# Three edits to a three-block layer kernel on Trainium2: recurrent-cell rows by DMA, an attention output projection by seven products, and a residual factor moved into a gate

## What is computed

```python
D = where(lower, b[:, None] - b[None, :] + i[None, :], -inf)
w_intra = exp(D - m_t[..., None])
w_inter = exp(inter - m_t)
s = einsum('bhtd,bhsd->bhts', q, k) * w_intra
num = s @ v + w_inter[..., None] * (q @ C)
```

## Time and profile before

| | |
|---|---|
| median of 3 runs | 4214.31 us (4209.85 to 4216.12) |
| the profiled execution, its own time | 4215.86 us |
| its span | 4214.1 us, mean granted clock 0.992 |
| PE | 4126.5 us busy, 98% of the span |
| PEld, DVE, ACT, POOL | 2128.0, 1640.6, 823.3, 787.9 us busy |
| chain that ended last | PE 91%, DVE 4%, ACT 1% |

### The profile page before, as it was taken

How to read it: one execution, slowest core, us unless ns; L and a number is a source line. 1 busy time by engine, 2 the same in 40 slices (tenths; PEclk the granted TensorE clock), 3 DMA queues, 4 the chain that set the end, 5 groups by cost and what they waited for, 6 DMA issues and landing times.

```text
span 4214.1 us, 46243 instructions
## 1 busy us (share of the span) xinstructions
PE 4126.5 (98%) x19608; PEld 2128.0 (50%) x19608; DVE 1640.6 (39%) x2754; ACT 823.3 (20%) x1612; POOL 787.9 (19%) x511
## 2 busy tenths in 40 slices
PE   8999999999999999999999999999999999999999
PEld 3466444444444456664444444654599344444444
DVE  3656263333333323331799431535433322222311
ACT  3124110000002113221332311633243100000000
POOL 3320052324230200000363200000100032212210
PEclk9999999999999999999999999999999999999999
DMA  5420011111111120000111121001100121111121
GB/s 203 169 79 11 30 41 49 40 50 40 40 50 46 75 80 18 28 16 30 40 40 40 40 80 50 31 28 46 61 4 24 40 80 50 40 41 50 61 94 34
DMA packets 53629, 218.50 MB, mean 52 GB/s; under 512 B 6192, under 2 KB 7728, under 8 KB 51504
## 3 DMA queue, kind: packets, MB, share of 16 engines
q1 hardware_dynamic: 47520, 167.53, 11.5%
q0 software_dynamic: 5904, 48.01, 3.0%
HBM read 194.50 MB, written 18.89 MB: 51 GB/s over the span
## 4 chain that ended last, share of the span: by engine, by line
PE 91%; DVE 4%; ACT 1%; issue 1%; DMA 1%; POOL 1%; SPq 0%; DVEq 0%; POOLq 0%; ACTq 0%
PE bank L718 34%; PE bank L184 27%; PE bank L3227 4%; PE bank L3045 4%; PE bank L2054 2%; PE bank L3238 2%; PE bank L2143 1%; PE bank L2113 1%; PE bank L501 1%; PE bank L2929 1%; PE bank L2913 1%; PE bank L2097 1%; PE bank L2134 1%; PE bank L2944 1%; PE bank L3168 1%
## 5 line engine op out<-in xcount | busy, mean ns | idle before, releaser
L184 PE MATMUL bank<-H,ring 128*128 128x512 f32 x1792 | 778.1, 595 | 6.7 <-DVE ABC L3558 2.9
L184 PEld LDWEIGHTS bank<-H,ring 128*128 128x128 f32 x1792 | 339.5, 191 | 435.2 <-issue 430.6
L184 PE MATMUL bank<-ABC,ring 128*128 128x512 f32 x944 | 412.0, 594 | 1.1 <-DVE ABC L1836 0.7
L718 PE MATMUL bank<-H,ring 128*128 128x512 f32 x736 | 323.6, 592 | 1.0 <-ACT ABC L2221 0.8
L184 PEld LDWEIGHTS bank<-ABC,ring 128*128 128x128 f32 x944 | 177.2, 190 | 225.6 <-issue 222.8
L2522 DVE SCALAR_TENSOR_TENSOR bank<-ABC,params,bank 128x1024 f32<-128x1024 f32 x184 | 237.3, 1290 | 8.0
L718 PEld LDWEIGHTS bank<-H,ring 128*128 128x128 f32 x736 | 139.6, 190 | 178.0 <-issue 178.0
L718 PE MATMUL bank<-X 128*128 128x512 f32 x400 | 181.6, 597 | 3.1 <-POOL X L708 3.1
L3045 PE MATMUL bank<-H 64*64 64x64 f32 x5088 | 169.3, 220 | 10.7 <-DVE H L3662 6.0
L718 PE MATMUL bank<-H,X 128*128 128x512 f32 x400 | 179.8, 592 | 0.0
L3045 PEld LDWEIGHTS bank<-H 64*64 64x64 f32 x5088 | 160.0, 136 | 15.7 <-issue 6.5
(11 more groups left out here) (686 smaller groups left out, 5866.4 us busy)
## 6 DMA issues: line engine op xcount, KB each, us to landing
ABC<-in_ada SPq DMA_DIRECT2D x48, 512.0 KB, 5.1
ring<-in_gu SPq DMA_DIRECT2D x44, 512.0 KB, 4.4
ring<-in_up SPq DMA_DIRECT2D x32, 512.0 KB, 4.1
ring<-in_down SPq DMA_DIRECT2D x32, 512.0 KB, 4.3
ring<-in_conv_in SPq DMA_DIRECT2D x24, 512.0 KB, 4.1
ring<-in_ffn SPq DMA_DIRECT2D x16, 704.0 KB, 4.9
ring<-in_proj SPq DMA_DIRECT2D x16, 512.0 KB, 5.2
ring<-in_mix SPq DMA_DIRECT2D x16, 512.0 KB, 4.4
```

The costliest lines, as they stand in the source:

```text
L184: mm = nc.tensor.matmul(bank[:, 2 * (m % 2) + h, :], ring[:, s % RING, k * P:(k + 1) * P], rhs(k)[:, h * HALF:(h + 1) * HALF], start=(k == ...
L718: mm = nc.tensor.matmul(S.bank(j, slot), lhs[:, k * P:(k + 1) * P], rhs[:, k, :], start=start and k == 0, stop=(k == 3), skip_group_check= ...
```

## The change

1. **Cell rows by DMA.** SP stores `r_r` and `r_wi` to a DRAM tensor `rows_kept` (ten small transfers), and for each cell reads them back spread over the partitions: one transfer of 256 KB into `weights_t`, two of 64 KB into `queries`, both now with three buffers. A cell's reads are issued once `out` of three cells before is done; the first three go ahead of tiles 2 and 3 of the mix. POOL adds the mask (`masked`), in place, in SBUF; DVE multiplies the queries in place, in SBUF. The lines 1187 and 1192 and `sel_head` are gone. The state's product uses banks 6 and 0 in turn and the small denominators have two buffers, so that two waits are one cell looser.
2. **Output projection.** Pairs 0 to 2 of `mla_out` run in the seven-product form, tiles 6 and 7 as before. The first product and the fifth of pair 0 are cut in half pairs of matmuls and put between the steps of the last head. POOL forms the operand sums for heads 0 to 6, DVE those for head 7. DVE adds joined blocks to X in a second operation, and the squares go to SBUF, not to a bank.
3. **The factor.** POOL's scaling of X by ALPHA is gone: the gate 1 + g1 is divided by ALPHA and the first norm behind it takes eps / ALPHA^2, which gives the same normalised value.

```diff
+            stream(sp, "dft")
+            stream(sp, "mix", 0, 2)
+            sp.wait_ge(*rows_dve.after(0, "r"))
+            sp.wait_ge(*rows_act.after(0, "r_wi"))
+            for d in range(2):
+                rows = slice(32 * d, 32 * d + 4)
+                sp.dma_start(rows_kept[0, d].rearrange("c h t -> h c t"), chunked(r_r)[rows]).then_inc(rows_saved, 16)
+                for e in range(2):
+                    for q in range(2):
+                        at = 32 * d + 2 * q + e
+                        sp.dma_start(rows_kept[1, d, :, 2 * e + q, :].unsqueeze(0), chunked(r_wi)[at:at + 1]).then_inc(rows_saved, 16)
+            sp.wait_ge(rows_saved, 16 + 160)
+            sp.wait_ge(*rows_pe.after(0, "em"))
+            sp.wait_ge(*rows_dve.after(0, "dec"))
+            for n in range(CELLS):
+                i, d, c, now = cell_of(n)
+                if n == 3:
+                    stream(sp, "mix", 2, 4)
+                if n >= 3:
+                    sp.wait_ge(*cell_pe.after(0, f"out{n - 3}"))
+                sp.dma_start(weights_t[n % 3], rows_kept[0, d, c].rearrange("h t -> (h t)").partition_broadcast(P)
+                             ).then_inc(rows_spread[n % 3], 16)
+                for e in range(2):
+                    sp.dma_start(queries[n % 3][64 * e:64 * e + 64], rows_kept[1, d, c, 2 * e:2 * e + 2, :].partition_broadcast(64)
+                                 ).then_inc(rows_spread[n % 3], 16)
+            stream(sp, "mix", 4)
...
+            def masked(n):
+                i, d, c, now = cell_of(n)
+                pool.wait_ge(*spread_of(n))
+                rows = weights_t[n % 3].rearrange("p (h t) -> p h t", h=4)
+                nc.gpsimd.tensor_tensor(rows, rows, causal[:, d:d + 1, :].broadcast_to([P, 4, P]), ALU.add
+                                        ).then_inc(*cells_pool.did(f"masked{n}"))
...
-            for m in range(DT):
-                last = nc.gpsimd.tensor_scalar(X[:, m, :], X[:, m, :], ALPHA_1, None, ALU.mult)
-            last.then_inc(*scaled_x.did("x1"))
...
-                    pe.wait_ge(*cell_dve.after(0, f"masked{n - 1}"))
-                for h in range(4):
-                    nc.tensor.matmul(bank[:, 0, h * P:(h + 1) * P], sel_head[:, 4 * d + h, :], r_r[:, now],
-                                     start=True, stop=True)
-                if n:
-                    pe.wait_ge(*cell_act.after(0, f"keys{n - 1}"))
-                for q in range(2):
-                    mm = nc.tensor.matmul(bank[:, 1, q * P:(q + 1) * P], sel_pair[:, 2 * d + q, :], r_wi[:, now], start=True, stop=True)
-                mm.then_inc(*cell_pe.did(f"bcast{n}"))
...
-                pe.wait_ge(*cell_dve.after(0, f"queries{n}"))
+                if n:
+                    pe.wait_ge(*cell_act.after(0, f"keys{n - 1}"))
...
-                    nc.vector.tensor_scalar(mod[:, 16:24], mod[:, 16:24], 1.0, None, ALU.add)
+                    nc.vector.tensor_scalar(mod[:, 16:24], mod[:, 16:24], 1.0, 1.0 / ALPHA_1, ALU.add, ALU.mult)
...
-                    v.wait_ge(*cell_pe.after(0, f"bcast{m}"))
-                    nc.vector.tensor_tensor(weights_t[m % 2].rearrange("p (h t) -> p h t", h=4), bank[:, 0, :].rearrange("p (h t) -> p h t", h=4),
-                                            causal[:, d:d + 1, :].broadcast_to([P, 4, P]), ALU.add).then_inc(*cell_dve.did(f"masked{m}"))
-                    nc.vector.tensor_tensor(queries[m % 2], A[:, 0:2, now], bank[:, 1, 0:256].rearrange("p (q t) -> p q t", q=2),
-                                            ALU.mult).then_inc(*cell_dve.did(f"queries{m}"))
+                    v.wait_ge(*spread_of(m))
+                    nc.vector.tensor_tensor(queries[m % 3], A[:, 0:2, now], queries[m % 3], ALU.mult
+                                            ).then_inc(*cell_dve.did(f"queries{m}"))
...
+            S = seven_out
+            nc.gpsimd.tensor_tensor(t1_out, quarter(B, 0, 1), quarter(B, 0, 0), ALU.subtract).then_inc(*rhs_out.did("t1"))
+            seven_lhs(pool, S, 0, "s1", "s2", "s3", "s4")
+            pool.wait_ge(*mla_dve.after(0, "gated7_6"))
+            nc.gpsimd.tensor_tensor(t3_out[:, 0:3], quarter(B, 1, 1)[:, 0:3], quarter(B, 0, 1)[:, 0:3], ALU.subtract
+                                    ).then_inc(*rhs_out.did("t3"))
+            pool.wait_ge(*mla_pe.after(0, "s7_7"))
+            pool.wait_ge(*rhs_out.after(0, "t3"))
+            nc.gpsimd.tensor_tensor(t2_out[:, 0:3], t3_out[:, 0:3], quarter(B, 0, 0)[:, 0:3], ALU.add).then_inc(*rhs_out.did("t2"))
+            pool.wait_ge(*rhs_out.after(0, "t2"))
+            nc.gpsimd.tensor_tensor(t4_out[:, 0:3], quarter(B, 1, 0)[:, 0:3], t2_out[:, 0:3], ALU.subtract).then_inc(*rhs_out.did("t4"))
+            for j in range(1, 3):
+                seven_lhs(pool, S, j, "s1", "s2", "s3", "s4")
+            pool.wait_ge(*rms_conv.summed.all())
...
+            def out_rest():
+                pe.wait_ge(*mla_dve.all())
+                pe.wait_ge(*mla_act.all())
+                pe.wait_ge(*taken("mla_heads"))
+                out_part(1, S.weights(0, 0, 1), out_b21, 0, 4).then_inc(products_done, 1)
+                pe.wait_ge(*rhs_out.after(0, "t2"))
+                pe.wait_ge(*last_head.after(0, "t2"))
+                pe.wait_ge(*S.lhs.after(0, "s2"))
+                out_part(2, out_s2, t2_out, 0, 4).then_inc(products_done, 1)
+                pe.wait_ge(*S.lhs.after(0, "s3"))
+                out_part(4, out_s3, t3_out, 0, 4).then_inc(*S.pe.did("p7"))
+                pe.wait_ge(*S.lhs.after(0, "s4"))
+                out_part(5, out_s4, out_b22, 0, 4).then_inc(*S.pe.did("p3"))
+                pe.wait_ge(*rhs_out.after(0, "t4"))
+                pe.wait_ge(*last_head.after(0, "t4"))
+                pe.wait_ge(*seven_out.after(0, "t22"))
+                seven_product(S, 0, 4, S.weights(0, 1, 1), t4_out, start=False).then_inc(products_done, 1)
...
+                    if not after and g == 7:
+                        out_first(0, 2)
                     if g >= 2:
                         out_turned(hd, g - 2)
                 if new_pair(after):
                     rotary_rows(after)
                 head_out(hd, 7)
+                if not after:
+                    out_first(2, 4)
                 out_turned(hd, 6)
+                if not after:
+                    out_fifth(0, 2)
                 if after:
                     key_rows(after, 0)
                     if new_pair(after):
                         rotary_turned(after)
                     key_rows(after, 1)
                 out_turned(hd, 7)
-            pe.wait_ge(*mla_dve.all())
-            pe.wait_ge(*taken("mla_heads"))
-            linear(pe, "mla_out", lambda k: B[:, k, :],
-                   between={(6, 1, 4): lambda: norm_stat(pe, rms_conv, 0), (7, 1, 2): lambda: norm_spread(pe, rms_conv, 0)})
+                if not after:
+                    out_fifth(2, 4)
...
+            out_rest()
+            out_free = lambda i, slot: seven_out.after(i, {3: "w", 4: "t21", 7: "t22"}[slot])
+            for j in (1, 2):
+                seven_products(pe, seven_out, j, out_rhs, out_free)
+            pe.wait_ge(*seven_out.after(2, "v"))
+            linear(pe, "mla_out", lambda k: B[:, k, :], 6,
+                   between={(7, 0, 0): lambda: pe.wait_ge(*taken("mla_out", 6)),
+                            (6, 1, 4): lambda: norm_stat(pe, rms_conv, 0), (7, 1, 2): lambda: norm_spread(pe, rms_conv, 0)})
...
+            for name, to, part, product, op in (("t3", t3_out, quarter(B, 1, 1), quarter(B, 0, 1), ALU.subtract),
+                                                ("t2", t2_out, t3_out, quarter(B, 0, 0), ALU.add),
+                                                ("t4", t4_out, quarter(B, 1, 0), t2_out, ALU.subtract)):
+                if name == "t3":
+                    v.wait_ge(*mla_dve.all())
+                else:
+                    v.wait_ge(*last_head.after(0, "t3" if name == "t2" else "t2"))
+                nc.vector.tensor_tensor(to[:, 3], part[:, 3], product[:, 3], op).then_inc(*last_head.did(name))
             v.wait_ge(middle_back, 16)
+            for j in range(3):
+                S = seven_out
+                p2, p6, p5, p7, p3 = (S.bank(j, n) for n in range(1, 6))
+                part, whole, turned_ = part_out[:, j % 2, :], whole_out[:, j % 2, :], turned_out[:, j % 2, :]
+
+                def final(product, base, m, h, to):
+                    name, dst = f"t{m + 1}{h + 1}", half_of(X, 2 * j + m, h)
+                    nc.vector.tensor_tensor(to, base, product, ALU.add).then_inc(*S.did(name, j))
+                    v.wait_ge(*S.after(j, name))
+                    nc.vector.tensor_tensor(dst, dst, to, ALU.add).then_inc(banks_free, 1)
+                v.wait_ge(*S.act.after(j, "p1"))
+                v.wait_ge(*S.done(j, 2))
+                final(p2, part, 0, 0, turned_)
+                v.wait_ge(*S.done(j, 3))
```

(31 more changed lines are left out.)

136 lines of the change are left out of this document (87 added, 49 removed).

## The result

| | before | after |
|---|---|---|
| median | 4212.08 us (4207.58 to 4216.12, 4 runs) | 4179.97 us (4175.94 to 4181.75, 4 runs) |
| profiled execution, its span | 4215.86, 4214.1 us | 4179.29, 4177.5 us |
| PE busy in it | 4126.5 us | 4086.2 us |

The ratio is 0.9923, 95% interval 0.9906 to 0.9940: 32.1 us faster by the medians. The forecast was 4184.6 us, with a range of 4177 to 4197.

A forecast was written before the change was run, and what follows sets the result against it. Cells and output projection were taken as PE-bound. Cells 18.1 + projection products 10.3 + last head's gaps 1.3 = 29.7 us off the profiled 4215.86 gave 4186.2; less 1.55 to the runs' median, 4184.6 us, range 4177 to 4197.

The forecast's parts named there:

- last head's gaps: Between the last head's steps: PE's idle 0.44, 0.47 and 0.38 us vanish behind eight matmuls put there, 1.3 us gained.
- The guard is held by POOL's mask: In the cells: a mask addition running over DVE's small guard operation (L1719) holds it; guard from 0.16 towards 0.6 us.
- The ring of DVE and ACT: In each cell: DVE's and ACT's steps from small denominator operations through copy, exponentials and multiply, put at 3.8 us.
- The ring through the transfer: In the cells: row reads, mask and output steps span three cells, L + 7.15, so 3.55 us each: not the bound.
- T: Cell time with a held guard: T = 3.8 + (L - 2.68)/2, taken as 4.2 us, bounds 3.8 and 4.9.
- mask misses the guard: Rival in the cells: no hold, by a tiny operation slipping through or late rows; cells 3.8 us, total 4179; chance 0.21.
- L: In the cells: time from a cell's rows leaving to their landing, taken as 3.5 us, between 2.6 and 4.8.
- the slow clock need not end earlier: First two cells, partly at 1.2 GHz: the slow stretch ends at the same time, so they give only 2 x 1.54 us.
- The statistics themselves: Behind cell 12: DVE's two head statistics stall the next cell; the change leaves that, 0 +-0.5 us.
- in front of p6 or p4: Projection's first pair: rival that the last head's operands are late, these products waiting some 2 us; 4187 us, chance 0.07.
- The low clock: Rival in the cells: waiting PE stays at 1.2 GHz, 6.9 us a cell, about 4223 us; chance 0.04.
- the late rows: Rival in the cells: short runs move worse, L of 6 to 8, cells 4.4 to 5.05 us; 4192 at 7; chance 0.20.

The follow-up runs named there:

- no_fill: Changed kernel with the eight products between the last head's steps moved behind them; 4178.74 us, one run.
- factor_alone: Kernel before with only the residual factor moved into gate and norm floor, POOL's scalings of X gone; 4215.55 us, ratio 1.0002 to before.
- guard_psum: Changed kernel with the guard and the step ahead of it made one step reading PSUM and SBUF; 4170.51 us, ratio 0.9902 to before.
- mask_dve: Changed kernel with the causal mask added on DVE instead of POOL, guard unchanged; 4176.37 us, ratio 0.9916 to before.
- late_rows: Changed kernel with the one-step PSUM guard, and a cell's rows asked for one cell later; 4206.44 us, one run.
- after_again: Changed kernel repeated, unedited, on one chip with the one-step guard version; 4182.21 us, ratio 0.9928 to before.
- cells_only: Changed kernel with the output projection as it was before, cells and factor changed; 4187.74 us, ratio 0.9945 to before.
- proj_only: Kernel before with only the output projection changed to seven products; 4205.35 us, ratio 0.9981 to before.
- guard_again: Changed kernel with the one-step PSUM guard, repeated beside the changed kernel on one chip; 4170.60 us, ratio 0.9900 to before.
- mask_dve_guard: Changed kernel with both the mask on DVE and the one-step PSUM guard; 4171.41 us, one run.
- halves: Changed kernel with POOL's mask addition cut into two halves of 128x256; 4176.49 us, one run.

## Why the prediction was right, step by step

| term | forecast | in the trace of after |
|---|---|---|
| up to cell 1, three broadcasts | 2 x 1.54 + 1.07 = 4.2 | 7.6 (286.55 to 304.19 before, 286.45 to 296.48 after) |
| cells 1 to 12, eleven | 11 x (5.27 - 4.2) = 11.8 | 10.8 (57.89 to 47.07) |
| cells 12 to 15, two | 2 x 1.07 = 2.1 | 0.3 (15.96 to 15.66) |
| the cells together | 18.1 | 18.7 |
| projection, products | 10.3 | 10.3 (99.67 to 89.34, no_fill) |
| last head's gaps | 1.3 | 1.9 |
| factor | 0 | 0 (factor_alone: -3 to +4 us by its interval) |
| sum | 29.7 | 30.9 (32.1 by the medians) |

**Right by mechanism.** The broadcasts are gone and PE's own cell is 5.27 - 1.54 = 3.73 us: guard_psum shows just that. The guard is held by POOL's mask, the step of which I was least sure: 1.16 us for 0.16 at 318.41. The rule of the Trainium skill (SBUF — State Buffer, SBUF: two separate sides), by which the one that starts first has the pair of ports for its whole instruction, holds here for four elements too. The ring of DVE and ACT, forecast 3.8, is 3.87 (mask_dve). The ring through the transfer was no bound, and late_rows shows it where it is one.

**Right on average, wrong in form: T.** The formula took a steady delay in every cell. In the trace some cells are free (3.87, the rival "mask misses the guard"), some are held for nearly the whole mask (4.8 to 4.9), and a few guards meet only its end (0.33 and 0.37 us). The mask's place drifts, since a held cell puts off the cells and not the rows that are under way. The rival's own condition, L of 3.9 or more, is met by the measured 4.0, but only just, which fits that both cases occur. Mean pitches of 4.17 to 4.35 in four traces (after, after_again, cells_only, no_fill) lie round the forecast 4.2; with the measured L of 4.0 the formula would have said 4.46. The guard reached 1.21 us, not 0.6. L itself (3.5 forecast) was too short because issue and landing of these rows were taken from other transfers: 0.54 for 0.33 us, 3.1 for 1.9.

**Wrong, two terms that cancel, and both are the clock.** First, "the slow clock need not end earlier": it did, at 291.1 us and not at 298.2. With 6.8 us less at the half clock 3.4 us are gained, and this is the whole of what the first stretch gave above 4.2. It recurs. With each execution's shift ahead of the cells taken off, cell 1 comes at 304.2 in before and factor_alone and at 305.7 in proj_only, with 10.2, 10.2 and 13.6 us at 0.50; in ten of the eleven kernels without the broadcasts it comes at 296.3 to 296.6, with 3.4 us at 0.50, and in mask_dve at 298.2, with 6.8. The factor is not the reason, as factor_alone has the 10.2 us of before. Why the clock rises sooner without the broadcasts was not tried and stays open: PE is busy without a gap in the low stretch in either kernel.

Second, behind cell 12 the two broadcasts gave 0.3 us instead of 2.1. The statistics themselves were put at 0 +-0.5, and about that held. What was left out is that TensorE's clock can fall behind a stall. In after PE stands 1.46 and 0.82 us (1.49 once before), and the clock is at 0.50 from 352.5 to 355.9; cell 14's products take 3.0 us for 1.7. In the four traces with a held guard the stretch from cell 12 to 14 gives 2.7 and 1.6 us where the clock has not fallen by cell 14 (cells_only, after_again), and 0.3 and 0.2 where it has (after, no_fill). A fall is not certain either: in after_again PE stands 1.43 and 0.81 us there, nearly as in after, and cell 14's products run at the full clock (1.13 us). It falls only at 359.1, and in guard_psum, guard_again, mask_dve_guard and halves not at all. The long queries product there (1.45 us for 0.42, at 347.75 on DVE) is held by the mask of cell 15 (POOL, from 347.65). With the guard freed, the three cells take 12.5 us instead of 15.7.

So the mechanisms of both edits were right, and that the total for the cells came out within a microsecond is partly luck: +3.4, -1.0 and -1.8 us.

**The projection** was sized right in its products. The gaps gave 1.9 us and not their 1.3: behind two of them the next PE step was also longer (1.13 for 0.89 us, 0.32 for 0.11), which is 0.45 more. The last 0.2 are not assigned to a row. Nothing stands in front of p6 or p4: PE is busy 68.00 of 68.00 us from 1882 to 1950.

**The rivals.** The low clock was given 0.04 and did not come in the steady cells of after: 1.00 from 298 to 340 us. late_rows shows that it and the late rows are one rival, not two: the priced 4.4 to 5.05 us a cell left out that an idle PE loses its clock.

**Beyond the projection.** The profiled executions stand 36.6 us apart at their ends, and 31.2 at 2060 us (0.3 of it ahead of the cells and between the two edits). The other 5.4 lie in code that is the same. In the same kernel's second trace that difference between 2060 us and the end is +1.3 (after_again), and in the others -8.7 (proj_only), -1.9 (guard_psum) and +0.8 to +4.5, so it belongs to the execution and not to the change.

## What to carry to other kernels

Taking PE work out of a PE-bound loop pays down to the next ring. Write the rings out beforehand, and look in each for a small DVE operation with two SBUF operands that a long GpSimd instruction can cover: reading one operand from PSUM took it out of the hold and gave 9 to 12 us here. Where TensorE may idle, give the sum a term for what its clock can lose, and take it as a range: the same stall cost it in some executions and not in others. Compare two executions just behind the change, not at their ends, and take off by how much they already differ just ahead of it. When a sum comes out, compare it stretch by stretch, and count for each stretch which pieces of the removed work lie in it.

## What the runs showed of the hardware

- An operation of 128x4 elements (0.16 us) with two SBUF operands took 1.16 to 1.21 us under a GpSimd addition of 1.27 us that had started first, and 0.73 at most under halves of 0.7 us; the same work with one operand in PSUM took 0.16 us under it (313.48 in guard_psum).
- 0.01 us decides: the guard that started that much ahead of the mask was free. So the mixture of free and held cells differs between executions, with a mean pitch of 4.28 and 4.35 us in two of the same kernel.
- A read of 64 KB spread over 64 partitions took SP 0.54 us to issue and landed after 3.1 us; another transfer of 64 KB needed 1.9.
- TensorE's idle times can cost twice: in after, PE stood 1.46 and 0.82 us and its next out products took 1.90 us for 1.13 at the 1.2 GHz level; in late_rows this recurs in every second cell, 1.45 us each time. In after_again, the same kernel, PE stood 1.43 and 0.81 us and the next out products took 1.13.
- The stretch at the 1.2 GHz level at the start of the cells was 10.2 us with the broadcast products and 3.4 us without them, in ten of eleven traces; PE was busy throughout in before and after.
